# A fused transformer forward pass on one core: delta rule in chunks of 128 tokens, and another deal of the modulation weight pieces

## The chip, the cores and the metric

The kernel is one program on one core of a Trainium2 chip. It is launched once and computes the whole function. The metric is the device time of that launch in microseconds, lower is better. The engines are PE (TensorE, matrix multiply), DVE (VectorE), ACT (ScalarE), POOL (GpSimd) and SP (SyncE, which here issues loads). Each runs its own instruction stream in order; they meet at semaphores.

## The reference

Two blocks run one after the other on 512 tokens of width 1024. The first is a hybrid block (a state space branch, a windowed attention branch, and a feed-forward network with a causal convolution of 3 taps). The second has two layers, each a feed-forward network, a token mixer and another feed-forward network. Its norms are scaled and shifted by a modulation, a matrix-vector product with a 1024 x 9216 matrix for each layer. The token mixer has a gated delta rule (4 heads of 128) beside a sparse attention. The parts that the change touches, cut to what matters:

```
mod = (cond @ ada_w[l] + ada_b[l]).reshape(B, 3, 3, D)

def chunk_gated_delta_rule(q, k, v, g, beta):
    """S_t = a_t S_{t-1}(I - b_t k_t k_t^T) + b_t v_t k_t^T, o_t = S_t q_t, in chunks."""
    C = GDN_CHUNK                                   # 64
    gc = jnp.cumsum(chunks(g), axis=-1)
    decay = exp(where(causal, gc[..., :, None] - gc[..., None, :], -inf))
    lower = where(strict, einsum("nbhcd,nbhsd->nbhcs", kb, kc) * decay, 0)
    u, w = split(triangular_solve(lower, [v * b, k * b * exp(gc)], unit_diagonal=True))
    def step(S, xs):
        v_new = u_i - w_i @ S
        o = (q_i * exp(g_i)) @ S + (q_i @ k_i.T * d_i) @ v_new
        S = S * exp(g_last) + (k_i * exp(g_last - g_i)).T @ v_new
        return S, o
```

The chunk length changes how the sum is grouped and not what it is: the recurrence over tokens is the same for any chunk length.

## The kernel before

All activations stay on the chip, features on the partitions and the 512 tokens along the free axis. The weights come as a stream of units of 128 x 2048 float32 (1 MB) through two buffers. For each unit SP loads `w_raw`, ACT copies it to `w_hi` (`split_unit`, L338), POOL subtracts to get `w_lo` (L331), and PE multiplies in three passes for float32 accuracy (`three_pass`, L344 to L346). The order of the stages is the list `PLAN`; inside a stage every engine has a function of its own (`pe_...`, `act_...`, `dve_...`) whose code order is its instruction order. No scheduler moves anything.

**Feed-forward** (`pe_ffn`, `act_ffn`, `dve_ffn`). The up stage has 22 units of 48 matmuls each, the down stage 16 units of 33 matmuls (every second one finishes a tile of `x`, L1264 or L1266). The first block's feed-forward (`conv` true) has for each up unit two convolutions of three DVE operations each (L1827, L1830), a multiplication (L1423) and a subtraction (L1411). In the other two kinds the up unit has one multiplication (L1428) and one subtraction.

**The modulation** of layer 0 is computed beside the first block's feed-forward, and that of layer 1 beside the first feed-forward of layer 0. Its weights come as 72 pieces of 128 x 1024 (0.5 MB) through the two slots of `ada_w`. ACT issues the load of piece n + 2 (`load`, L1334) once DVE has released piece n (`ada_free`). DVE runs four operations of 128 x 256 for each piece (L1392, L1394, L1396 or L1402) with a wait on each. After two pieces PE sums over the partitions with two small matmuls (L1302). `ada_turns` says how many pieces belong to each unit. It is the table that all three engines read:

```
        if conv:
            n = (2 if u % 11 == 10 else 1) if u < NUP else 3
        else:
            n = 2 if u < NUP + 14 else 0
```

Here NUP is 22 (up units) and NDN is 16 (down units). At a stage's end `modulated` (L1449) turns the sums into the gains and shifts that the next norm uses, and the norm starts at L449.

**The delta rule** (`pe_gdn`, `act_gdn`, `dve_gdn`). `m_U` becomes the transposed inverse of a unit triangular matrix. It starts from blocks of 2, and each step `b` doubles the block length: 16 matmuls L1665, ACT copies (L1803), 16 matmuls L1674 and 16 matmuls L1678, DVE subtractions (L1935, L1937). The last step leaves L1674 out. The matmuls always cover whole blocks of 128 x 128, whatever `b` is; four heads by four blocks of 128 tokens make 16. Then L1684 forms `m_nw`, and the recurrence goes over 8 chunks of 64 tokens. Even chunks lie in partitions 0 to 63 and odd ones in 64 to 127. In each chunk, for each of four heads, PE makes `v_new` (L1698 with 64 rows and 64 columns of the array, L1700 with 128 rows and 64 columns), ACT copies it to `t_vn` (L1811), PE makes the state's increment (L1708) and two parts of the output (L1705, L1710), DVE updates the state `m_S` (L1946, the first time a copy, L1949) and copies the output out (L1951). Behind the recurrence ACT squares the output (L1815), PE sums the squares over the partitions (L1717, 16 matmuls with one moving column), DVE and ACT turn them into factors (L1960 to L1967), and PE spreads these (L1723). The sparse attention stage then starts with a weight unit (L344).

## Time and profile before

| what | value |
|---|---|
| times of three runs, us | 4437.58, 4438.89, 4424.72 |
| median, us | 4437.58 |
| the profiled execution, us | 4410.95 |
| its span in the trace, us | 4409.1 |
| granted PE clock, mean over the span | 0.908 |
| PE busy / DVE / ACT / POOL, us | 4192.4 / 1718.3 / 1382.6 / 1355.5 |

The profiled execution lies 26.6 us under the median of the runs. The span is the time from the first to the last instruction of the trace; 1.9 us of the execution lie around it. The granted clock is a share of 2.4 GHz: 1.00 is 2.4 GHz and 0.50 is 1.2 GHz. Each matmul of plain float32 shows as two instructions in the trace, so 16 of them are x32.

### The profile page before, as it was taken

How to read it: one execution, taken by the hardware profiler on the slowest of the kernel's cores; microseconds unless marked ns; L12 is line 12 of the kernel's file. 1: busy time of each engine (PE TensorE's matmuls, PEld its weight loads, DVE VectorE, ACT ScalarE, POOL GpSimd, SP SyncE). 2: the span in 40 equal slices, each digit the busy share in tenths (PEclk: the TensorE clock that was granted, in tenths of full speed). 3: DMA queues.
4: the chain of work that ended last, by engine and by line, in shares of the span. 5: the costliest groups of instructions: out<-in, count | busy, mean ns of one | idle time of the engine just before them, and what ended most of it. 6: DMA issues, size and time to landing. Idle time of an engine off the chain costs nothing.

```text
span 4409.1 us, 50418 instructions
## 1 busy us (share of the span) xinstructions
PE 4192.4 (95%) x20328; PEld 3448.1 (78%) x20328; DVE 1718.3 (39%) x3207; ACT 1382.6 (31%) x1872; POOL 1355.5 (31%) x298
## 2 busy tenths in 40 slices
PE   7999999999998899999979999999999998899998
PEld 7887888877887788888866678878888886667887
DVE  4767245534765544545334321011103532432110
ACT  4556234433221222233212232232223321222222
POOL 2223432223443344532010034454453201003445
PEclk9999999999998899989965599999998977559999
DMA  3111221112446555721110022332232102002223
GB/s 126 60 66 70 95 86 58 48 58 93 145 155 229 181 185 183 249 89 49 32 45 1 1 86 96 114 106 97 100 129 86 49 6 72 1 1 77 96 105 124
DMA packets 66355, 401.92 MB, mean 91 GB/s; under 512 B 7776, under 2 KB 8288, under 8 KB 27872
## 3 DMA queue, kind: packets, MB, share of 16 engines
q1 hardware_dynamic: 44624, 314.73, 20.2%
q10 hardware_dynamic: 21520, 84.16, 6.1%
q8 instruction: 159, 2.61, 0.2%
q14 instruction: 52, 0.43, 0.0%
HBM read 396.76 MB, written 2.10 MB: 90 GB/s over the span
## 4 chain that ended last, share of the span: by engine, by line
issue 76%; POOL 14%; PE 9%; POOLq 0%; DVE 0%; ACT 0%; DVEq 0%; ACTq 0%
POOL w_lo L331 14%; PE g L344 3%; PE g L346 3%; PE g L345 3%; PE p L405 0%; POOLq L327 0%; DVE x L1463 0%; PE p L429 0%; POOLq L330 0%; POOLq L331 0%; ACT L421 0%; ACT n_sq L413 0%; DVE h_lo L466 0%; DVE n_t L462 0%; ACT h_hi L443 0%
## 5 line engine op out<-in xcount | busy, mean ns | idle before, releaser
L331 POOL TENSOR_TENSOR w_lo<-w_raw,w_hi 128x2048 fp32r<-128x2048 f32 x294 | 1355.3, 4610 | 3043.4 <-ACT w_hi L338 3043.4
L344 PE MATMUL g<-h_hi,w_lo 128*128 128x512 f32 x2848 | 1134.9, 398 | 20.8 <-DVE h_lo L466 12.4
L346 PE MATMUL g<-h_hi,w_hi 128*128 128x512 f32 x2848 | 1116.0, 392 | 0.0
L345 PE MATMUL g<-h_lo,w_hi 128*128 128x512 f32 x2848 | 1115.2, 392 | 0.0
L338 ACT ACTIVATE w_hi<-w_raw 128x2048 fp32r<-128x2048 f32 x294 | 562.6, 1914 | 1236.7 <-PE g L346 1211.1
L344 PEld LDWEIGHTS g<-h_hi,w_lo 128*128 128x128 f32 x2848 | 539.3, 189 | 141.2 <-issue 21.3
L346 PEld LDWEIGHTS g<-h_hi,w_hi 128*128 128x128 f32 x2848 | 538.7, 189 | 115.0
L345 PEld LDWEIGHTS g<-h_lo,w_hi 128*128 128x128 f32 x2848 | 539.6, 189 | 113.4 <-issue 4.1
L344 PE MATMUL g<-act_hi,w_lo 128*128 128x512 f32 x880 | 358.6, 407 | 0.0
L345 PE MATMUL g<-act_lo,w_hi 128*128 128x512 f32 x880 | 352.9, 401 | 0.0
L346 PE MATMUL g<-act_hi,w_hi 128*128 128x512 f32 x880 | 352.8, 401 | 0.0
L1428 DVE TENSOR_TENSOR p<-f_acc,g 128x512 f32<-128x512 f32 x88 | 61.3, 696 | 621.8 <-PE g L346 621.8
L1266 DVE SCALAR_TENSOR_TENSOR x<-g,mods,x 128x512 f32<-128x512 f32 x48 | 36.0, 751 | 475.1 <-PE g L346 475.1
L346 PEld LDWEIGHTS g<-act_hi,w_hi 128*128 128x128 f32 x880 | 168.5, 191 | 40.9
L345 PEld LDWEIGHTS g<-act_lo,w_hi 128*128 128x128 f32 x880 | 169.2, 192 | 38.6
L344 PEld LDWEIGHTS g<-act_hi,w_lo 128*128 128x128 f32 x880 | 169.3, 192 | 38.5
L1394 DVE SCALAR_TENSOR_TENSOR p<-ada_w,csilu,p 128x256 f32<-128x256 f32 x360 | 176.3, 490 | 48.5 <-DMA ada_w<-in_ada 36.5
L2082 PEld LDWEIGHTS p<-m_v,n_pt 128*128 128x128 f32 x640 | 140.2, 327 | 53.9 <-issue 49.1
L2082 PE MATMUL p<-m_v,n_pt 128*128 128x64 f32 x640 | 150.1, 422 | 31.5 <-ACT n_pt L2200 31.5
L2061 PE MATMUL g<-n_k,n_q 64*128 64x128 f32 (+3 forms) x256 | 157.8, 767 | 2.7 <-ACT n_pct L2192 1.6
L2186 ACT ACTIVATE n_p<-g,n_stat 128x128 f32<-128x128 f32 (+3 forms) x128 | 67.4, 527 | 292.6 <-DVE n_stat L2309 292.6
L1359 ACT ACTIVATE f_acc<-g 128x512 f32<-128x512 f32 x88 | 52.8, 600 | 277.5 <-PE g L346 277.5
(390 smaller groups left out, 5347.6 us busy)
## 6 DMA issues: line engine op xcount, KB each, us to landing
w_raw<-in_stream SPq DMA_DIRECT2D x294, 1024.0 KB, 4.8
ada_w<-in_ada ACTq DMA_DIRECT2D x144, 512.0 KB, 4.4
n_w<-in_w ACTq DMA_DIRECT2D x8, 1024.0 KB, 14.1
x<-in_x SPq DMA_DIRECT2D x4, 512.0 KB, 7.1
out_x<-x SPq DMA_DIRECT2D x4, 512.0 KB, 2.6
masks<-in_masks SPq DMA_DIRECT2D x1, 1408.0 KB, 13.2
cols<-in_cols SPq DMA_DIRECT2D x1, 338.0 KB, 13.0
n_pos<-in_pos ACTq DMA_DIRECT2D x1, 256.0 KB, 6.6
```

The lines of the kernel that those rows point to most:

```text
L331: K.nc.gpsimd.tensor_tensor(K.w_lo[:, s], K.w_raw[:, s], K.w_hi[:, s].bitcast(F32), ALU.subtract).then_inc(K.sem("w_lo"), 1)
L338: act.activation(K.w_hi[:, s], K.w_raw[:, s], ACT.Copy).then_inc(K.sem("w_hi"), 1)
L344: nc.tensor.matmul(out, w_lo, h_hi, start=start, stop=False)
L345: nc.tensor.matmul(out, w_hi, h_lo, start=False, stop=False)
L346: return nc.tensor.matmul(out, w_hi, h_hi, start=False, stop=stop)
L1266: v.scalar_tensor_tensor(x, K.g[b][:], gate(m), x, ALU.mult, ALU.add).then_inc(K.sem("x_ready"), 1)
L1359: act.activation(K.f_acc[:, s], K.g[2 * s][:], ACT.Silu).then_inc(K.sem("f_s"), 1)
L1394: v.scalar_tensor_tensor(acc, w, c, acc, ALU.mult, ALU.add).then_inc(pos.own, pos.tick())
L1428: v.tensor_tensor(K.p[s][:], K.f_acc[:, s], K.g[2 * s + 1][:], ALU.mult).then_inc(K.sem("f_u"), 1)
L2061: t.matmul(K.g[2 * (v % 2) + i][:, 0:w], K.n_q[r, j, qb * P:qb * P + P], K.n_k[r, 2 + i, 0:w], start=True, stop=True).then_inc(K.sem("scor ...
L2082: last = t.matmul(K.p[2 + v % 2][:, 64 * i:64 * i + 64], K.n_pt[:, v % 2, 4 * i + k], K.m_v[:, k, P * i + 64 * G:P * i + 64 * G + 64], sta ...
L2186: act.activation(K.n_p[:, v % 2, i * w:i * w + w], K.g[2 * (v % 2) + i][:, 0:w], ACT.Exp, scale=-1.0, bias=s[:, v % 4, i:i + 1], accum_out ...
```

## The change

Two things change. `ada_turns(True)`, the deal for the first block's feed-forward, gives two pieces to each of the 22 up units and the first 12 down units, and one to each of the last four, in place of one (twice two) in the up stage and three in the down stage. The number of pieces stays 72, and the deal of the other feed-forward stays as it is.

The delta rule goes in 4 chunks of 128 tokens. The masks follow (`tri` for `tri64`, `ones` for `bd64`, `causal` for `off64`, a new `inv64`), the inversion has a further step (b = 64; b = 32 becomes a whole step), and the recurrence has 4 passes, all of whose matmuls use 128 rows and 128 columns of the array. The output of all chunks stays in the PSUM banks `g[h]`. It is squared and multiplied from there, so that the copies of L1951 go; the last chunk has no state update; and the sums of squares go to `p[3]`.

```
--- before.py
+++ after.py
@@ -1282,7 +1282,7 @@
     turns, at = [], 0
     for u in range(NUP + NDN):
         if conv:
-            n = (2 if u % 11 == 10 else 1) if u < NUP else 3
+            n = 2 if u < NUP + 12 else 1
         else:
             n = 2 if u < NUP + 14 else 0
...
@@ -1588,9 +1588,9 @@
     def spread(h):
         if h:
             pe.wait_ge(K.sem("m_qe"), pos.next("m_qe"))
-        t.matmul(K.p[0][:], K.mask("off64"), ident.unsqueeze(1).broadcast_to([P, NB, P]), start=True, stop=False)
+        t.matmul(K.p[0][:], K.mask("causal"), ident.unsqueeze(1).broadcast_to([P, NB, P]), start=True, stop=False)
         for c in range(NB):
-            last = t.matmul(K.p[0][:, c * P:c * P + P], K.m_gl[:, c, h:h + 1].broadcast_to([P, P]), K.mask("tri64"),
+            last = t.matmul(K.p[0][:, c * P:c * P + P], K.m_gl[:, c, h:h + 1].broadcast_to([P, P]), K.mask("tri"),
                             start=False, stop=c == NB - 1)
         last.then_inc(K.sem("m_bc"), 1)
...
@@ -1624,8 +1624,8 @@
     unit(0)
     pe.wait_ge(K.sem("m_gl"), pos.next("m_gl"))
     g = K.m_gl[:].rearrange("p c h -> p (c h)")
-    t.matmul(K.p[0][:, 0:16], K.mask("tri64"), g, start=True, stop=True)
-    t.matmul(K.p[1][:, 0:16], K.mask("bd64"), g, start=True, stop=True).then_inc(K.sem("acs"), 1)
...
-    for b in (2, 4, 8, 16, 32):
+    for b in (2, 4, 8, 16, 32, 64):
...
@@ -1668,7 +1668,7 @@
             if b == 2:
                 pe.wait_ge(K.sem(f"g_free{h}"), pos.next(f"g_free{h}"))
             pe.wait_ge(K.sem("m_copied"), pos.next("m_copied"))
-            if b < 32:
+            if b < 64:
                 for c in range(NB):
                     q = slice(c * P, c * P + P)
                     last = t.matmul(K.g[h][:, q], K.m_U[:, h, q], K.t_y[:, h, q], start=True, stop=True)
@@ -1684,37 +1684,28 @@
             last = t.matmul(K.p[h][:, q], K.m_kbe[:, h, q], K.m_U[:, h, q], start=True, stop=True)
         last.then_inc(K.sem("m_raw"), 1)
 
-    for ch in range(8):
-        c, e = ch // 2, ch % 2
-        r = slice(64 * e, 64 * e + 64)
+    for c in range(NB):
         q = slice(c * P, c * P + P)
-        qe = slice(c * P + 64 * e, c * P + 64 * e + 64)
-        o = slice(64 * e, 64 * e + 64)
         for h in range(4):
-            if ch == 0:
-                pe.wait_ge(K.sem("m_copied"), pos.next("m_copied"))
-            else:
-                pe.wait_ge(K.sem("m_st"), pos.next("m_st"))
-            last = t.matmul(K.p[h][r, 0:P], K.m_U[r, h, qe], K.m_vb[r, h, q], start=True, stop=ch == 0)
-            if ch:
-                last = t.matmul(K.p[h][r, 0:P], K.m_nw[:, h, qe], K.m_S[:, h], start=False, stop=True)
+            pe.wait_ge(K.sem("m_st" if c else "m_copied"), pos.next("m_st" if c else "m_copied"))
+            last = t.matmul(K.p[h][:, 0:P], K.m_U[:, h, q], K.m_vb[:, h, q], start=True, stop=c == 0)
+            if c:
+                last = t.matmul(K.p[h][:, 0:P], K.m_nw[:, h, q], K.m_S[:, h], start=False, stop=True)
             last.then_inc(K.sem("m_raw"), 1)
         for h in range(4):
-            if ch:
-                pe.wait_ge(K.sem("m_os"), pos.next("m_os"))
-                t.matmul(K.g[h][:, o], K.m_S[:, h], K.m_qk[:, h, qe], start=True, stop=False)
-        for h in range(4):
+            if c:
+                t.matmul(K.g[h][:, q], K.m_S[:, h], K.m_qk[:, h, q], start=True, stop=False)
             pe.wait_ge(K.sem("m_copied"), pos.next("m_copied"))
-            t.matmul(K.p[h][:, 256:256 + P], K.m_kd[r, h, q], K.t_vn[r, h], start=True, stop=True
-                     ).then_inc(K.sem("m_step"), 1)
-            t.matmul(K.g[h][:, o], K.t_vn[r, h], K.m_at[r, h, qe], start=ch == 0, stop=True
-                     ).then_inc(K.sem("m_step"), 1)
-    pos.skip("m_os", 4)
-    pos.skip("m_st", 4)
+            if c < NB - 1:
+                t.matmul(K.p[h][:, 256:256 + P], K.m_kd[:, h, q], K.t_vn[:, h], start=True, stop=True
+                         ).then_inc(K.sem("m_step"), 1)
+            last = t.matmul(K.g[h][:, q], K.t_vn[:, h], K.m_at[:, h, q], start=c == 0, stop=True)
+            if c == NB - 1:
+                last.then_inc(K.sem("m_os"), 1)
     for h in range(4):
         pe.wait_ge(K.sem("m_osq"), pos.next("m_osq"))
         for c in range(NB):
-            last = t.matmul(K.g[0][:, h * NB + c:h * NB + c + 1], K.m_sq[:, h, c * P:c * P + P], K.mask("ones")[:, 0:1],
...
@@ -1797,22 +1788,20 @@
     for h in range(4):
         act.wait_ge(K.sem("m_raw"), pos.next("m_raw"))
         act.activation(K.t_T[:, h], K.p[h][:], ACT.Copy).then_inc(K.sem("m_copied"), 1)
-    for b in (2, 4, 8, 16, 32):
+    for b in (2, 4, 8, 16, 32, 64):
         for h in range(4):
             act.wait_ge(K.sem("m_raw"), pos.next("m_raw"))
             act.activation(K.t_y[:, h], K.p[h][:], ACT.Copy).then_inc(K.sem("m_copied"), 1)
     for h in range(4):
         act.wait_ge(K.sem("m_raw"), pos.next("m_raw"))
         act.activation(K.m_nw[:, h], K.p[h][:], ACT.Copy, scale=-1.0).then_inc(K.sem("m_copied"), 1)
-    for ch in range(8):
-        r = slice(64 * (ch % 2), 64 * (ch % 2) + 64)
+    for c in range(NB):
         for h in range(4):
             act.wait_ge(K.sem("m_raw"), pos.next("m_raw"))
-            act.activation(K.t_vn[r, h], K.p[h][r, 0:P], ACT.Copy).then_inc(K.sem("m_copied"), 1)
-    pos.skip("m_os", 28)
+            act.activation(K.t_vn[:, h], K.p[h][:, 0:P], ACT.Copy).then_inc(K.sem("m_copied"), 1)
     for h in range(4):
         act.wait_ge(K.sem("m_os"), pos.next("m_os"))
-        act.activation(K.m_sq[:, h], K.m_o[:, h], ACT.Square).then_inc(K.sem("m_osq"), 1)
+        act.activation(K.m_sq[:, h], K.g[h][:], ACT.Square).then_inc(K.sem("m_osq"), 1)
     pos.skip("m_ss", 4)
     act.wait_ge(K.sem("n_ms"), pos.next("n_ms"))
...
@@ -1928,39 +1917,31 @@
         decayed(h)
     for h in range(4):
         v.tensor_tensor(blocks(K.t_m[:, h]), blocks(K.t_l[:, h]), mask("inv2"), ALU.mult).then_inc(K.sem("m_inv"), 1)
-    for b in (2, 4, 8, 16, 32):
+    for b in (2, 4, 8, 16, 32, 64):
         for h in range(4):
-            if b < 32:
+            if b < 64:
                 dve.wait_ge(K.sem("m_step"), pos.next("m_step"))
                 v.tensor_tensor(K.t_T[:, h], K.t_T[:, h], K.g[h][:], ALU.subtract).then_inc(K.sem("m_inv"), 1)
             dve.wait_ge(K.sem("m_step"), pos.next("m_step"))
             v.tensor_tensor(K.m_U[:, h], K.m_U[:, h], K.p[h][:], ALU.subtract).then_inc(K.sem("m_inv"), 1)
-            if b < 32:
+            if b < 64:
                 v.tensor_tensor(blocks(K.t_m[:, h]), blocks(K.t_l[:, h]), mask(f"inv{2 * b}"), ALU.mult
                                 ).then_inc(K.sem("m_inv"), 1)
-    for ch in range(8):
-        c, e = ch // 2, ch % 2
+    for c in range(NB - 1):
         for h in range(4):
             dve.wait_ge(K.sem("m_step"), pos.next("m_step"))
-            if ch:
-                v.scalar_tensor_tensor(K.m_S[:, h], K.m_S[:, h], K.m_el[:, h, ch:ch + 1], K.p[h][:, 256:256 + P],
+            if c:
+                v.scalar_tensor_tensor(K.m_S[:, h], K.m_S[:, h], K.m_el[:, h, c:c + 1], K.p[h][:, 256:256 + P],
                                        ALU.mult, ALU.add).then_inc(K.sem("m_st"), 1)
             else:
                 v.tensor_copy(K.m_S[:, h], K.p[h][:, 256:256 + P]).then_inc(K.sem("m_st"), 1)
-            dve.wait_ge(K.sem("m_step"), pos.next("m_step"))
-            v.tensor_copy(K.m_o[:, h, c * P + 64 * e:c * P + 64 * e + 64],
-                                   K.g[h][:, 64 * e:64 * e + 64]).then_inc(K.sem("m_os"), 1)
-    dve.wait_ge(K.sem("m_os"), pos.next("m_os", 32))
     for h in range(4):
-        x = K.m_o[:, h]
         dve.wait_ge(K.sem("m_osq"), pos.next("m_osq"))
-        v.scalar_tensor_tensor(x, x, K.col2("gdn_norm"), K.m_z[:, h], ALU.mult, ALU.mult
-            ).then_inc(pos.own, pos.tick())
+        v.scalar_tensor_tensor(K.m_o[:, h], K.g[h][:], K.col2("gdn_norm"), K.m_z[:, h], ALU.mult, ALU.mult
+                               ).then_inc(K.sem(f"g_free{h}"), 1)
     dve.wait_ge(K.sem("m_ss"), pos.next("m_ss", 12))
-    v.scalar_tensor_tensor(K.m_f[:], K.g[0][:, 0:16], 1.0 / P / P, K.m_rq2[:].rearrange("p h c -> p (h c)"),
+    v.scalar_tensor_tensor(K.m_f[:], K.p[3][:, 0:16], 1.0 / P / P, K.m_rq2[:].rearrange("p h c -> p (h c)"),
                            ALU.mult, ALU.mult).then_inc(K.sem("n_ms"), 1)
-    for b in range(4):
-        dve.sem_inc(K.sem(f"g_free{b}"), 1)
     dve.wait_ge(K.sem("n_std"), pos.next("n_std"))
     v.reciprocal(K.m_f[:], K.m_f[:]).then_inc(pos.own, pos.tick())
...
@@ -2472,12 +2455,12 @@
 def masks():
     i, j = np.arange(P)[:, None], np.arange(P)[None, :]
     m = {"ident": i == j, "ones": i >= 0 * j, "tri": i <= j, "bd64": i // 64 == j // 64,
-         "tri64": (i <= j) & (i // 64 == j // 64)}
-    for b in (1, 2, 4, 8, 16, 32):
+         }
+    for b in (1, 2, 4, 8, 16, 32, 64):
         m[f"inv{b}"] = (i < j) & (i // b != j // b) & (i // (2 * b) == j // (2 * b))
```

The instruction order on DVE, in the first block's up stage, from the multiplication L1423 of one unit to that of the next (f_acc holds the convolutions, csilu the condition vector). Before:

```order
L1423 TENSOR_TENSOR p<-f_acc,p 128x512
L1392 TENSOR_SCALAR p<-ada_w,csilu 128x256
L1394 SCALAR_TENSOR_TENSOR p<-ada_w,csilu,p 128x256 x2
L1396 SCALAR_TENSOR_TENSOR p<-ada_w,csilu,p 128x256
L1411 TENSOR_TENSOR act_lo<-p,act_hi 128x512
L1827 TENSOR_SCALAR f_acc<-g,cols 128x512
L1830 SCALAR_TENSOR_TENSOR f_acc<-g,cols,f_acc 128x511
L1830 SCALAR_TENSOR_TENSOR f_acc<-g,cols,f_acc 128x510
L1827 TENSOR_SCALAR f_acc<-g,cols 128x512
```

The same place in the changed kernel:

```order
L1423 TENSOR_TENSOR p<-f_acc,p 128x512
L1392 TENSOR_SCALAR p<-ada_w,csilu 128x256
L1394 SCALAR_TENSOR_TENSOR p<-ada_w,csilu,p 128x256 x2
L1396 SCALAR_TENSOR_TENSOR p<-ada_w,csilu,p 128x256
L1394 SCALAR_TENSOR_TENSOR p<-ada_w,csilu,p 128x256 x3
L1402 SCALAR_TENSOR_TENSOR ada_acc<-ada_w,csilu,p 128x256
L1411 TENSOR_TENSOR act_lo<-p,act_hi 128x512
L1816 TENSOR_SCALAR f_acc<-g,cols 128x512
L1819 SCALAR_TENSOR_TENSOR f_acc<-g,cols,f_acc 128x511
L1819 SCALAR_TENSOR_TENSOR f_acc<-g,cols,f_acc 128x510
L1816 TENSOR_SCALAR f_acc<-g,cols 128x512
```

Four more operations of 128 x 256 stand between the multiplication and the subtraction in every unit (L1827 and L1830 are L1816 and L1819 in the changed file).

The instruction order on PE in the recurrence, from the last of a chunk's four heads in the making of v_new to the outputs of the first two heads (m_S is the state, t_vn is v_new). Before, chunk of 64 tokens:

```order
L1698 MATMUL p<-m_vb,m_U 64x128
L1700 MATMUL p<-m_S,m_nw 64x128
L1705 MATMUL g<-m_qk,m_S 128x64 x4
L1708 MATMUL p<-t_vn,m_kd 128x128
L1710 MATMUL g<-m_at,t_vn 128x64
L1708 MATMUL p<-t_vn,m_kd 128x128
L1710 MATMUL g<-m_at,t_vn 128x64
```

In the changed kernel, chunk of 128 tokens:

```order
L1691 MATMUL p<-m_vb,m_U 128x128
L1693 MATMUL p<-m_S,m_nw 128x128
L1697 MATMUL g<-m_qk,m_S 128x128
L1700 MATMUL p<-t_vn,m_kd 128x128
L1702 MATMUL g<-m_at,t_vn 128x128
L1697 MATMUL g<-m_qk,m_S 128x128
L1700 MATMUL p<-t_vn,m_kd 128x128
L1702 MATMUL g<-m_at,t_vn 128x128
```

The state's part of the output (L1705, now L1697) moved from a group of four ahead of the others to the place just ahead of each head's own pair, and every output has 128 columns.

## Rows read from the trace of the kernel before

**Rows 1.** The profile's page, busy time, share of the span and instructions of PE.

```profile
PE 4192.4 (95%) x20328; PEld 3448.1 (78%) x20328; DVE 1718.3 (39%) x3207; ACT 1382.6 (31%) x1872; POOL 1355.5 (31%) x298
```

**Rows 2.** Windows: stretch, length, busy time (instructions) by engine, granted clock, DMA share, GB/s.

```profile
1071.20:1305.30 234.10, 234.10 (x1055) 194.27 (x1054) 168.17 (x260) 66.39 (x65) 97.02 (x21) 1.00 0.42 144
1305.30:1488.00 182.70, 160.21 (x677) 131.37 (x676) 100.60 (x201) 35.29 (x25) 73.55 (x16) 0.88 0.64 224
1515.00:1755.00 240.00, 240.00 (x1097) 199.42 (x1096) 111.27 (x210) 63.58 (x64) 97.03 (x21) 1.00 0.56 183
1755.00:1890.00 135.00, 135.00 (x644) 111.50 (x643) 65.27 (x129) 35.42 (x24) 72.58 (x16) 1.00 0.69 233
```

**Rows 3.** Waits of 1380 to 1560 us: engine, line, releaser, total us, times, longest.

```profile
DVE p L1394 <- DMA ada_w<-in_ada: 20.2, 10, 3.6
```

**Rows 4.** Timeline of DVE, first up stage: start, us, instruction, [idle before, releaser].

```profile
1171.44 0.81 DVE L1827 TENSOR_SCALAR f_acc<-g,cols 128x512 f32<-128x512 f32 x1 [3.06 <-PE g L346]
...
1182.33 0.81 DVE L1827 TENSOR_SCALAR f_acc<-g,cols 128x512 f32<-128x512 f32 x1 [2.58 <-PE g L346]
...
1191.21 1.53 DVE L1830 SCALAR_TENSOR_TENSOR f_acc<-g,cols,f_acc 128x511 f32<-128x511 f32 x2
...
1193.71 0.81 DVE L1827 TENSOR_SCALAR f_acc<-g,cols 128x512 f32<-128x512 f32 x1 [0.97 <-PE g L346]
```

**Rows 5.** Timeline of DVE, first down stage, its start and end.

```profile
1305.01 0.81 DVE L1827 TENSOR_SCALAR f_acc<-g,cols 128x512 f32<-128x512 f32 x1 [2.58 <-PE g L346]
...
1487.34 0.69 DVE L1264 TENSOR_TENSOR x<-x,g 128x512 f32<-128x512 f32 x1 [0.91 <-PE g L346]
...
1500.23 0.19 DVE L449 TENSOR_REDUCE n_ms<-p 128x4 f32<-128x32 f32 x1 [1.03 <-PE p L405]
```

**Rows 6.** Timeline of DVE, second down stage (layer 0), its start and end.

```profile
1757.23 0.70 DVE L1428 TENSOR_TENSOR p<-f_acc,g 128x512 f32<-128x512 f32 x1 [5.54 <-PE g L346]
...
1893.69 0.75 DVE L1266 SCALAR_TENSOR_TENSOR x<-g,mods,x 128x512 f32<-128x512 f32 x1 [12.18 <-PE g L346]
...
1898.78 0.19 DVE L449 TENSOR_REDUCE n_ms<-p 128x4 f32<-128x32 f32 x1 [3.44 <-PE p L405]
```

**Rows 7.** Timeline of PE, two inversion steps of layer 0.

```profile
2079.46 3.74 PE L1665 MATMUL p<-t_T,t_m 128*128 128x128 f32 x32
...
2090.18 3.74 PE L1665 MATMUL p<-t_T,t_m 128*128 128x128 f32 x32
```

**Rows 8.** Timeline of layer 0, recurrence over chunks and what follows it.

```profile
2122.43 1.19 PE L1698 MATMUL p<-m_vb,m_U 64*64 64x128 f32 x8
...
2123.55 0.48 PE L1708 MATMUL p<-t_vn,m_kd 64*128 64x128 f32 x2
...
2124.07 0.29 DVE L1949 COPY m_S<-p 128x128 f32<-128x128 f32 x1 [4.41 <-PE p L1708]
...
2125.48 0.43 PE L1698 MATMUL p<-m_vb,m_U 64*64 64x128 f32 x2
...
2131.32 0.43 PE L1698 MATMUL p<-m_vb,m_U 64*64 64x128 f32 x2
...
2170.22 6.99 PE L1717 MATMUL g<-masks,m_sq 128*128 128x1 f32 x32
...
2178.31 5.66 PE L1723 MATMUL p<-masks,m_fac 128*128 128x128 f32 x32 [1.10 <-DVE m_fac L1967]
...
2183.72 0.48 PE L344 MATMUL g<-h_hi,w_lo 128*128 128x512 f32 x1
```

**Rows 9.** Timeline of PE, layer 1, the same: recurrence's start and next stage's first matmul.

```profile
3556.41 1.19 PE L1698 MATMUL p<-m_vb,m_U 64*64 64x128 f32 x8
...
3631.17 0.48 PE L344 MATMUL g<-h_hi,w_lo 128*128 128x512 f32 x1
```

**Rows 10.** Windows of 20 us: inversion in layer 0, recurrence in layer 1.

```profile
2080.00:2100.00 20.00, 20.00 (x181) 20.00 (x180) 13.30 (x23) 4.78 (x8) 0.00 (x0) 1.00 0.00 1
...
3580.00:3600.00 20.00, 20.00 (x78) 14.64 (x78) 4.35 (x16) 2.11 (x8) 0.00 (x0) 0.50 0.00 1
```

15 lines of the change are left out of this document (10 added, 5 removed).

## The prediction

> **What bounds the kernel now.** I read the page first. PE is busy for 95% of the span, the next engine for 39% [rows 1]. So the question at each place is whether PE is fed, and which work it gets. The windows by stage answer it for the feed-forwards. In the first up stage, the second up stage and the second down stage PE is busy all the time at the full clock of 2.4 GHz (granted 1.00). In the first down stage it is busy for 160.2 of 182.7 us, at a granted clock of 0.88, with DMA at 224 GB/s [rows 2]. The waits name the cause there: DVE waits for modulation pieces to land, ten times and up to 3.6 us each, for L1394 alone [rows 3]. Two slots hold the pieces, a load starts only when its slot is released, and three pieces per unit are more than that pair of slots turns over in a unit. ACT issues the loads in its own order, so the next split waits too, and then PE.
>
> The second place is the delta rule. In the inversion PE passes 181 instructions per 20 us at the full clock. In layer 1's recurrence it passes 78 at a granted clock of 0.50, which is 1.2 GHz [rows 10]. Layer 0 takes 61.3 us from the recurrence's first matmul to the next stage's first (2122.43 to 2183.72) [rows 8]. Layer 1 takes 74.8 us for the same instructions (3556.41 to 3631.17) [rows 9]. PE sets the end in both places, so times on PE are times of the kernel.
>
> **The deal, down stage.** After the change 12 units have two pieces and four have one, 28 in all. The second feed-forward has 28 pieces in the same 16 units, same loads, same matmuls. From the last up unit's end to the last tile of x it needs 136.46 us (1757.23 to 1893.69) [rows 6], the first 182.33 (1305.01 to 1487.34) [rows 5]. The gain is 45.9 us. Behind the last tile come 12.89 us to the next norm's first operation now [rows 5], against 5.09 in the second [rows 6]. Three pieces and their waits stand in between now, and one will; its four operations and two matmuls run beside ACT's last square. I take 5.3 us. That gains 7.6 us.
>
> **The deal, up stage.** A unit with one piece and no sum on PE lasts 10.89 us (1171.44 to 1182.33), one with a sum 11.38 (1182.33 to 1193.71) [rows 4]. Before, 11 sums fell between the first and last up unit, now 21. Ten more at 0.49 us cost 4.8 us. Does DVE keep up? The unit at 1182.33 is one of the two that already have two pieces. DVE ended its chain at about 1192.75 (1191.21 and 1.53) and then waited 0.97 us for PE [rows 4]. So DVE needs 10.42 of 11.38 us, nothing is carried into the next unit, and the extra 20 pieces lie beside PE. The cover is 0.97 us a unit. Without it each unit would cost what exceeds it. The loads run at 183 GB/s in the second up stage, which already has two pieces a unit, and PE is fed [rows 2]. What is queued behind ACT's waits for a free slot is the next unit's silu, whose input comes only at 1192.75. The deal together: 45.9 + 7.6 - 4.8 = 48.7 us.
>
> **The inversion's added step.** Two steps start 10.72 us apart [rows 7], for 48 matmuls, 0.223 us each. b = 32 becomes a whole step and the short last step stays short, so one whole step is added: 10.7 us in each layer, on PE, at the full clock. Masks, `m_el` and the sums' masks change no instruction's size: nothing.
>
> **The recurrence.** All its matmuls become 128 x 128 blocks, as in the inversion; I price them at 0.223 us. The first chunk: 1.12 us until L1708 can start (2122.43 to 2123.55) [rows 8], then eight matmuls, 1.8 us. The two middle ones have 20 each, 4.47 us. The last has 16, 3.57 us. That is 15.4 us. Two waits could stand in between. From a head's product to its copy being ready pass at most 0.9 us (the first chunk's 1.12 less one matmul), and the last head's copy is wanted 2.2 us after its product. The state of the last head has its product started 4.0 us into a chunk and is read 5.8 us after the chunk's start; from product to DVE's start 0.52 us pass (2123.55 to 2124.07) and the operation lasts about 0.3 [rows 8]. Both are hidden. Before, the same part would last 3.05 us (2122.43 to 2125.48) and seven times 5.84 (2125.48 to 2131.32) [rows 8], 43.9 us at the full clock; it lasted 47.8 in layer 0 (to 2170.22), and more in layer 1.
>
> Then the tail. L1717 took 6.99 us [rows 8] at half clock; at the full one I halve it, 3.5 us. ACT's four squares, from PSUM now, overlap the end of the recurrence and each is ready before PE wants it. The chain to the factors is 1.1 us (6.99 after 2170.22, to 2178.31) [rows 8]. L1723 is 16 matmuls, 3.6 us instead of 5.4. Sum: 15.4 + 3.6 + 1.1 + 3.6 = 23.7 us. With the added step 34.4 us. Layer 0 gains 61.3 - 34.4 = 26.9 us, layer 1 74.8 - 34.4 = 40.4 us.
>
> The unknown cost is the price of a matmul in this mix. Its lower bound is the inversion's 0.223 us, its upper that of the old chunk, 5.84 us for 20, 0.292 each [rows 8]. With the upper one the middle chunks stay at 5.84 and the last takes 4.67, 3.8 us more per layer, 7.6 in all. I take the lower: the new matmuls have the inversion's rows and columns of the array, while the old ones alternate between 64 and 128 rows (64*64, 64*128) [rows 8]. The Trainium skill, "TensorEngine Tiling (Array Packing)", Key Properties, says that a change of tiling mode drains the engine. By that rule the old chunk's excess over 20 times 0.223, 1.4 us, is drains, none are left, and the sum stands at the lower value; if the excess came from waits for other engines instead, the sum would be up to 7.6 us smaller. No row before shows which.
>
> The clock: in the trace it was full through the inversion and fell in the recurrence, whose chunk passes 40 instructions in 5.84 us at the full clock, 137 in 20 us, many with 64 rows or columns. The new one has the inversion's 180, so I let it stay full. The tail has 3.5 us of matmuls with one moving column and 1.1 us of nothing, so it may fall there, as it had in layer 0 before (L1717 took 0.44 us per matmul, twice the 0.223). That costs between 0 and 7 us per layer (L1717 and L1723 at twice their time). I take 2 us each.
>
> **The sum.** 48.7 + 26.9 + 40.4 - 4 = 112 us. Against the profiled execution, 4410.95, that gives 4299 us. The median of the runs, 4437.58, lies 26.6 us above that execution. Part of such a spread can be the recurrence itself: its 13.5 us between two layers of equal work are clock alone, and a run in which the clock falls at its start pays more still. What is lost there goes with the change. What is lost elsewhere stays, 4326 us. I take the middle, 4312.
>
> **The rivals**, each counted from 4424, the middle between the execution and the median.
> A. The clock falls in the new recurrence too, at its start. For: it fell in both layers in the old one. Against: the density just named. Then 23.7 us nearly double in both layers, 45 us, 60 with the upper price of a matmul. Gain 56 to 71, time 4353 to 4368.
> B. The first up stage becomes bound by DVE and its loads. For: the cover is only 0.97 us. Against: the unit of [rows 4] has it all. If loads came as late as in the first down stage (182.33 us for 48 pieces, 3.8 each), a unit would last 7.6 us for two pieces and about 6.2 for the convolutions and the rest (10.42 less some 4.2 for two pieces), 13.8, so 22 units lose some 53 us. Gain about 59, time 4365.
> C. The other side: the gaps that such late pieces open let PE's clock fall through the whole up stage, as it did at times in the first down stage (0.88). The 48 matmuls of a unit at 1.2 GHz cost 10.9 us more, 22 units 240. About 4552, slower. It decides from 11 units on. Against: 1.00 in both up stages [rows 2].
> D. Two pieces per unit leave the first down stage bound by loads after all, and half of the 45.9 us stays: 4335. Against it the second down stage moves 233 GB/s and PE is fed [rows 2].
> E. The change does not do what it says: the 112 us cancel against costs not seen, and the time stays within 13 us of before. Both parts would have to fail at once.
>
> The Trainium skill, "TensorE: Matmul & The Clock Gate", HAM oscillation, says that gaps in PE's work bring the throttle back. By that rule A needs gaps that the sum above does not find, and C needs B first; the trace agrees so far, with 0.88 in the stage that waits and 1.00 in the three that do not [rows 2].
>
> **How the numbers follow.** The forecast as summed has 0.75, with its own range 4288 to 4338. A has 0.11, D 0.06, B 0.05, C 0.02, E 0.01. Leaving out the lower and upper ends, 8 in 10 lie from 4286 to 4350; the bounds of the matmul's price (7.6), the tail (up to 10 more) and the median's offset (13 each way) are in it. 0.3%, 13 us, is about what a measurement of this kernel tells from no change. Faster: all but C and E, 0.97. Same 0.01, slower 0.02.
>
> **What would show it.** The first down stage lasts 136 to 138 us, DVE's waits for `ada_w` go, and the granted clock there is 1.00. Up units come every 11.4 us with DVE idle about 1 us in each. There are six inversion steps where there were five, 10.7 us apart. A middle chunk lasts 4.5 us with a granted clock of 1.00, and recurrence plus tail 24 to 27 us in both layers, which become alike. If a middle chunk lasts 5 us or more at the full clock, the price of a matmul was wrong. If the up units last over 11.5, the cover was. If layer 1 still takes 10 us more than layer 0, the clock was.

## The result, and the profile after

| kernel | median, us | lowest to highest (runs) |
|---|---|---|
| before | 4431.15 | 4407.34 to 4438.89 (4) |
| changed | 4298.01 | 4297.66 to 4298.11 (4) |

The ratio is 0.971, with a 95% interval of 0.967 to 0.975: 3% faster. The profiled executions took 4410.95 and 4298.11 us, 112.8 apart. The forecast was 4312 us with a range of 4286 to 4350, and a sum of 112.

The page of the changed kernel, PE's row, answers to [rows 1]. PE is still the bound.

```profile
PE 4104.6 (96%) x20184; PEld 3393.1 (79%) x20184; DVE 1711.2 (40%) x3127; ACT 1378.1 (32%) x1848; POOL 1355.4 (32%) x298
```

Its windows (columns as in [rows 2]): first up stage, first down stage, inversion and recurrence in layer 0, and the tail behind it.

```profile
1069.90:1309.10 239.20, 239.20 (x1094) 198.78 (x1093) 206.46 (x340) 65.77 (x65) 97.00 (x21) 1.00 0.51 183
1309.00:1446.40 137.40, 136.44 (x645) 111.73 (x643) 65.07 (x129) 35.62 (x25) 73.80 (x16) 1.00 0.66 227
2080.00:2100.00 20.00, 19.98 (x180) 19.79 (x178) 6.07 (x16) 6.74 (x21) 0.00 (x0) 1.00 0.00 1
2100.90:2112.00 11.10, 10.00 (x67) 9.92 (x66) 4.87 (x10) 3.78 (x7) 0.00 (x0) 0.69 0.01 1
```

The first down stage lasts 137 us where it had 183, at a clock of 1.00 where it had 0.88. PE passes 180 instructions in 20 us across the end of the inversion and the recurrence, at 1.00; only the tail falls, to 0.69. The timeline of DVE, with the answers to [rows 4] and [rows 5]:

```profile
1138.38 0.81 DVE L1816 TENSOR_SCALAR f_acc<-g,cols 128x512 f32<-128x512 f32 x1 [0.98 <-PE g L346]
...
1149.76 0.81 DVE L1816 TENSOR_SCALAR f_acc<-g,cols 128x512 f32<-128x512 f32 x1 [0.98 <-PE g L346]
...
1309.08 0.81 DVE L1816 TENSOR_SCALAR f_acc<-g,cols 128x512 f32<-128x512 f32 x1 [0.98 <-PE g L346]
...
1323.60 1.54 DVE L1394 SCALAR_TENSOR_TENSOR p<-ada_w,csilu,p 128x256 f32<-128x256 f32 x3 [3.42 <-DMA ada_w<-in_ada]
...
1446.38 0.69 DVE L1264 TENSOR_TENSOR x<-x,g 128x512 f32<-128x512 f32 x1 [7.04 <-PE g L346]
...
1453.16 0.19 DVE L449 TENSOR_REDUCE n_ms<-p 128x4 f32<-128x32 f32 x1
```

Up units come 11.38 us apart, with 0.98 us of idle time on DVE. Its waits for `ada_w`, 72.3 us in 33 before by the view of waits over the whole span, are 11.5 us in 5. The stage lasts 239.2 us (1069.91, the first unit's first tile, to 1309.08), 5.0 more than before (1070.84 to 1305.01). From there to the last tile of x it is 137.30 us, and to the norm 6.78. The timeline of PE answers to [rows 8] and [rows 9]:

```profile
2063.98 3.74 PE L1665 MATMUL p<-t_T,t_m 128*128 128x128 f32 x32
...
2074.70 3.74 PE L1665 MATMUL p<-t_T,t_m 128*128 128x128 f32 x32
...
2085.42 1.34 PE L1691 MATMUL p<-m_vb,m_U 128*128 128x128 f32 x8
...
2092.85 0.39 PE L1691 MATMUL p<-m_vb,m_U 128*128 128x128 f32 x2
...
2097.32 0.39 PE L1691 MATMUL p<-m_vb,m_U 128*128 128x128 f32 x2
...
2100.89 4.53 PE L1708 MATMUL p<-masks,m_sq 128*128 128x1 f32 x32
2106.52 5.60 PE L1714 MATMUL p<-masks,m_fac 128*128 128x128 f32 x32 [1.10 <-DVE m_fac L1948]
...
2111.87 0.48 PE L344 MATMUL g<-h_hi,w_lo 128*128 128x512 f32 x1
```

Inversion steps are 10.72 us apart, and there are six. A middle chunk lasts 4.47 us, the four 15.47, the tail 10.98, together 26.45 us in layer 0 and the same in layer 1 (3495.02 to 3521.47).

The rest is seen best from norm to norm, by the start of L449. One row per execution; the first stretch is the first block's feed-forward, the third and sixth hold the two delta rules.

| profiled execution | us between norms |
|---|---|
| before | 447.2, 398.5, 670.5, 381.2, 382.5, 683.8, 381.1 |
| changed | 401.6, 398.3, 645.9, 381.2, 382.5, 643.0, 381.1 |

### The profile page after: what moved, and what is told of

Its sections match the earlier page's. It is cut to its first block, busy times and chain, and to the rows that moved or that the text cites. A ratio compares the mean times of both kernels' runs of the same rounds, so it can differ in the third digit from the quotient of the medians.

```text
span 4296.3 us, 50018 instructions
## 1 busy us (share of the span) xinstructions
PE 4104.6 (96%) x20184; PEld 3393.1 (79%) x20184; DVE 1711.2 (40%) x3127; ACT 1378.1 (32%) x1848; POOL 1355.4 (32%) x298
## 4 chain that ended last, share of the span: by engine, by line
issue 76%; POOL 14%; PE 9%; POOLq 0%; DVE 0%; ACT 0%; DVEq 0%; ACTq 0%
POOL w_lo L331 14%; PE g L344 3%; PE g L345 3%; PE g L346 3%; PE p L405 0%; POOLq L327 0%; DVE x L1463 0%; PE p L429 0%; POOLq L330 0%; POOLq L331 0%; ACT L421 0%; ACT n_sq L413 0%; DVE h_lo L466 0%; DVE n_t L462 0%; ACT h_hi L443 0%
## 5 line engine op out<-in xcount | busy, mean ns | idle before, releaser
L345 PEld LDWEIGHTS g<-h_lo,w_hi 128*128 128x128 f32 x2848 | 539.4, 189 | 112.8 <-issue 4.1
## 6 DMA issues: line engine op xcount, KB each, us to landing
masks<-in_masks SPq DMA_DIRECT2D x1, 1344.0 KB, 13.2
```

The source lines that it names most:

```text
L345: nc.tensor.matmul(out, w_hi, h_lo, start=False, stop=False)
```

## The experiments

Each group ran beside the kernel before on one chip; the groups ran on different chips.

**One part at a time.** The new line of `ada_turns` in the kernel before, and the old line in the changed one:

```
-            n = (2 if u % 11 == 10 else 1) if u < NUP else 3
+            n = 2 if u < NUP + 12 else 1
```

> The kernel before with the new deal of the modulation pieces alone; the delta rule stays in chunks of 64. My theory: the parts add up. The deal gave 45.5 us between the second norm of the first block and the first norm of layer 0 in the profiled executions (447.2 and 401.6 us), so the profile here shows 402 us for that stretch, a first down stage of 137 us (1309 to 1446), and the median stands 45 to 49 us under the kernel before. The runs spread as before, by 15 to 30 us, since the old recurrence, whose clock I hold responsible, is still in it. Rival one, the gains overlap (the clock or the DMA of one part helps the other): the stretch shows less than 35 us or more than 55. Rival two, the spread of the kernel before came from the three pieces per unit and not from the recurrence: the runs here lie within 2 us of each other.

> The changed kernel with the old deal of the modulation pieces; the delta rule stays in chunks of 128. My theory: 61 to 68 us less than the kernel before, of which 24.6 in layer 0 and 37.7 in layer 1 by the profiled executions (recurrence and tail 26.5 us in both layers, against 61.3 and 74.8), the rest of it the part of the old recurrence's clock that varies from run to run. The runs lie within 2 us of each other. The first down stage stays at 182 us with waits for ada_w of 72 us in all. Rival, the spread comes from the first down stage: the runs here spread by 15 to 30 us.

The deal alone: 4382.50 us (4374.71 to 4385.01, 4 runs) against 4429.38 for the kernel before on that chip (13 runs, 4412.83 to 4439.50), ratio 0.990 (0.987 to 0.993), 46.9 us. The stretch is 401.95 us, the down stage 137.65. The chunks alone: 4342.57 us (4340.82 to 4344.05, 4 runs), ratio 0.981 (0.979 to 0.984), 86.8 us, where I expected 61 to 68. The two gains sum to 133.7 us; the change gave 133.1 between its medians. So the parts add up, and the chunks are worth some 20 us more in a typical run than in the profiled execution. The two sets of runs also say where the spread comes from. With the old recurrence and the new deal it is 10.3 us, less than the 15 to 30 that I expected and far over the 2 of rival two. With the new recurrence and the old deal it is 3.2 us, over the 2 expected and far under the 15 to 30 of the rival. So most of the spread needs the old recurrence.

**The kernel before once more.**

> The kernel before, profiled again. My theory of its run-to-run spread (4407 to 4439 us): it lies in the recurrence, where the clock falls at a place that varies. Then every stretch between norms has the length it had (within 1 us) except the two that hold the delta rule (670.5 and 683.8 us in the first profile), and their difference from the first profile is that of the executions. Rival: the difference lies in the first down stage (447.2 us from norm to norm in the first profile), whose loads can come in another order.

Its eight runs had a median of 4427.09 us (4413.18 to 4435.30). The profiled one took 4418.21 us, 7.3 more than the first profile. From norm to norm: 442.8, 398.2, 683.7, 381.2, 382.3, 683.7, 381.1. Layer 0's stage is 13.2 us longer and the first stretch 4.4 shorter. The timeline of PE in layer 0's recurrence:

```profile
2131.32 0.43 PE L1698 MATMUL p<-m_vb,m_U 64*64 64x128 f32 x2
...
2137.17 0.43 PE L1698 MATMUL p<-m_vb,m_U 64*64 64x128 f32 x2
...
2146.83 0.68 PE L1698 MATMUL p<-m_vb,m_U 64*64 64x128 f32 x2
...
2157.26 0.68 PE L1698 MATMUL p<-m_vb,m_U 64*64 64x128 f32 x2
```

A chunk goes from 5.85 to 10.43 us (2146.83 to 2157.26) once the clock is down. Here it fell in the fifth chunk in both layers. In layer 0 of the first profile it fell only near the end of the recurrence; with the deal alone it fell in the fourth chunk of layer 0. Six such stages took 670.5, 683.8, 683.7, 683.7, 687.9 and 683.7 us, so the first is the exception. The old first stretch varied too: 447.2 and 442.8 in the two profiles of before, 444.2, 451.1, 444.8 and 441.1 in the profiles of four other kernels with the old deal; with the new deal it stayed between 399.5 and 403.9. So the theory that every other stretch keeps its length within 1 us was wrong, and the rival has a share: 4.4 us between two executions of the same kernel, against 13.2 from layer 0's delta rule. Both profiles of before lie under its median of 4429.38. Of the 86.8 us that the chunks gave, the two stages account for 65 by the first profile and for 78 by the second; where the other 8 lie no profile shows.

**What makes an old chunk slow.** Three kernels with 8 chunks whose matmuls cover more of the array. They leave out the limits of a chunk of 64 tokens, so what they compute differs from the reference; their times are what is asked. Full blocks:

```
-            last = t.matmul(K.p[h][r, 0:P], K.m_U[r, h, qe], K.m_vb[r, h, q], ...)
+            last = t.matmul(K.p[h][:, 0:P], K.m_U[:, h, q], K.m_vb[:, h, q], ...)
...
-            t.matmul(K.g[h][:, o], K.t_vn[r, h], K.m_at[r, h, qe], ...)
+            t.matmul(K.g[h][:, 0:P], K.t_vn[:, h], K.m_at[:, h, q], ...)
```

and in the same way for the other three. With full rows only, `r` goes on the side of the operands and `qe` and `o` stay (the first chunk keeps its 64 rows in L1708 and L1710); with full columns only it is the reverse.

> The kernel before, still 8 chunks of 64 tokens, but every matmul of the recurrence (the two of v_new, the two of the output, the state's increment) and the copy of v_new cover 128 rows and 128 columns of the array. What is computed in the recurrence differs from the reference by that; the number of instructions, of waits and their order do not. Theory one, the old chunk's 5.84 us (20 matmuls, 0.292 each) against the new one's 4.47 (0.223 each) is the alternation of 64 and 128 rows and columns: a chunk takes 4.5 us here and the recurrence from its first matmul to the sums of squares 34 to 35 us in place of 47.8 in layer 0. Theory two, the excess is waits for ACT and DVE between the dependent steps, which eight chunks have and four do not show because DVE no longer copies the output out: a chunk stays at 5.8 us. On the clock: if it falls because 64-row matmuls leave the array half used, it stays at 1.00 through the recurrence here and both layers are alike, with runs within 2 us of each other; if it falls for another reason (the number of chunks), it falls at about the same place, to 0.50.

> The kernel before, 8 chunks of 64 tokens, with all its matmuls of the recurrence from chunk 1 on summing over 128 rows of the array (v_new's first product, the state's increment and the second part of the output took 64), while the columns of v_new and the moving columns of the outputs stay 64. What is computed in the recurrence differs from the reference by that. Full blocks throughout gave 4.47 us for a chunk in place of 5.84 and a clock that stayed at 1.00. Theory one, it is the change between 64 and 128 rows that costs: a chunk takes 4.5 us or less here (two of its five kinds of matmuls have fewer moving columns), and the clock stays at 1.00. Theory two, it is the 64 columns: a chunk stays near 5.8 us and the clock falls at about the fourth chunk.

> The kernel before, 8 chunks of 64 tokens, whose matmuls of the recurrence have all 128 stationary and moving columns, while three of its five kinds still sum over 64 rows of the array. What is computed in the recurrence differs from the reference by that. With full rows and the old columns a chunk took 4.71 us, with both full 4.47, with neither 5.84 until the clock fell. Theory one, the alternation of 64 and 128 rows is what costs and what goes with the lower clock: a chunk stays at 5.8 us or more while the clock is full, the clock falls at the fourth or fifth chunk, and the two delta rule stages take 683 us or more from norm to norm. Theory two, rows and columns count alike: a chunk takes about 5.1 us and the clock falls later or not at all, with stages of 655 to 665 us.

| recurrence | chunk, us | two delta rule stages, us | median, us (runs) |
|---|---|---|---|
| old (64 rows and columns) | 5.85, later 10.43 | 670.5 to 687.9 | 4429.38 (13) |
| full columns only | 5.79 | 663.5, 663.4 | 4383.31 (2) |
| full rows only | 4.71 | 652.9, 653.0 | 4359.38 (2) |
| full blocks | 4.47 | 653.1, 653.0 | 4364.14 (4) |

Full blocks do 2.5 times the multiplications (rows times columns times moving columns, over the 20 matmuls) with the same instructions and waits in 4.47 us a chunk. So the 1.37 us over 4.47 were not waits. (The 5 us between its median and that of full rows lie in the old first stretch, 451.1 and 444.8 us.) The rows name the place. Timeline of PE with full columns only, inside a chunk:

```profile
2137.06 0.48 PE L1698 MATMUL p<-m_vb,m_U 64*128 64x128 f32 x2
2137.48 0.49 PE L1700 MATMUL p<-m_S,m_nw 128*128 128x128 f32 x2
2137.89 0.48 PE L1698 MATMUL p<-m_vb,m_U 64*128 64x128 f32 x2
...
2141.00 0.38 PE L1708 MATMUL p<-t_vn,m_kd 64*128 64x128 f32 x2
2141.23 0.38 PE L1710 MATMUL g<-m_at,t_vn 64*128 64x128 f32 x2
2141.45 0.38 PE L1708 MATMUL p<-t_vn,m_kd 64*128 64x128 f32 x2
```

Where matmuls of 64 and 128 rows alternate, they start 0.42 us apart; where two of 64 rows follow each other, 0.22. A change costs 0.19 us here, and 0.17 on the mean of the eight changes of a chunk (5.79 less 4.47). With the old columns it cost 0.14: L1698 and L1700 started 0.36 us apart, and 0.22 with full rows; eight such changes make 1.1 us, the difference between 5.84 and 4.71. The last 0.24 us, from 4.71 to 4.47, go with the 64 columns. That settles the term that the prediction left between two bounds: the alternation of rows is 1.1 of the 1.4 us of excess, and the Trainium skill's rule cited there ("TensorEngine Tiling (Array Packing)", Key Properties) holds with these numbers.

The table also says how much of the chunk change is the chunk length. A stage of 683.7 us becomes 653.1 with full blocks and eight chunks, 30.6 us less, and 643.0 to 646.0 in the changed kernel, 7 to 10 less again: half as many chunks, less the added inversion step. So three quarters or more of the gain of such a stage come from matmuls that all cover the whole array (no change of rows, and a clock that holds), and the smaller part from fewer chunks.

The clock is a second thing. In none of the three did it fall in the profiled recurrence. Windows of the recurrence, full columns only, and the kernel before in layer 0 and twice in layer 1:

```profile
2119.00:2159.00 40.00, 40.00 (x278) 33.23 (x276) 12.19 (x55) 7.76 (x29) 0.00 (x0) 1.00 0.00 1
2126.00:2160.00 34.00, 34.00 (x234) 25.21 (x234) 9.96 (x44) 6.53 (x24) 0.00 (x0) 1.00 0.00 1
3560.00:3578.00 18.00, 18.00 (x124) 13.21 (x122) 5.46 (x24) 3.45 (x13) 0.00 (x0) 1.00 0.00 1
3578.00:3632.00 54.00, 52.90 (x224) 42.08 (x223) 14.65 (x43) 10.17 (x25) 0.00 (x0) 0.53 0.00 1
```

Theory one of the text on full columns was right on the price and wrong on the clock: the alternation is there in full, 5.79 us a chunk, and the clock stayed at 1.00. PE is shown busy all the time in the first three; in layer 1 the clock fell at 3578 us behind 18.00 us without a gap, and the last window has 1.1 us of nothing only in the tail. In the kernel before the weight loads are busy for 25.2 of 34 us, with full columns for 33.2 of 40. The two runs with full columns, 4377.36 and 4389.26, are 12 us apart, and only the first was profiled; their mean granted clocks, 0.914 and 0.913, do not tell whether it fell in the second. What exactly the clock follows stays open.

**The cover of the up stage.**

```
-            n = 2 if u < NUP + 12 else 1
+            n = 3 if u < 24 else 0
```

> The changed kernel with three modulation pieces in each of the 22 up units and the first two down units, none behind them. It asks how far the cover of the up stage reaches. A unit has 11.38 us of matmuls plus 0.25 for half a sum more; DVE needs 10.42 us with two pieces, and about 2.1 more for the third. Theory one, DVE's own work is the bound: units of 12.5 us, the up stage 275 us in place of 239, the down stage about 133, the kernel some 30 us over 4298, and the granted clock stays at or near 1.00. Theory two, the turnover of the two slots is the bound, as in the first down stage before the change (182.7 us for 48 pieces, 3.8 each): a unit lasts three times 3.8 and 6.2, some 17.6 us, the up stage 387 us, and the clock falls in it: over 150 us more.

4373.39 us (2 runs), 70 more than the changed kernel on that chip (below), between the theories. The first stretch took 473.4 us. A unit on DVE, and a window of the stage (columns as in [rows 2]):

```profile
1185.28 0.80 DVE L1816 TENSOR_SCALAR f_acc<-g,cols 128x512 f32<-128x512 f32 x1
...
1196.73 0.49 DVE L1392 TENSOR_SCALAR p<-ada_w,csilu 128x256 f32<-128x256 f32 x1 [1.66 <-DMA ada_w<-in_ada]
...
1199.44 0.80 DVE L1816 TENSOR_SCALAR f_acc<-g,cols 128x512 f32<-128x512 f32 x1
```

```profile
1150.00:1250.00 100.00, 87.81 (x373) 72.31 (x372) 81.22 (x139) 21.24 (x21) 31.71 (x8) 0.91 0.53 184
```

A unit takes 14.2 to 14.7 us, this one 14.16: DVE's own work of 12.5 and a wait of 1.66 for the third piece, since two slots hold two. The clock in the stage fell to 0.91, not further. So the bound is DVE plus one load's rest, and theory two had put all three loads in series. The cover is worth what [rows 4] show: two pieces fit, three cost 3 us a unit.

**The rest of the down stage.** Two other deals:

```
+            n = 2 if u < NUP + 14 else 0                                 # flat
+            n = 1 if NUP <= u < NUP + 2 else 2 if u < NUP + 15 else 0    # late
```

> The changed kernel, whose first feed-forward deals two pieces to each of the first 14 down units and none to the last two, as the second feed-forward does, in place of two to 12 and one to four. My theory: what stood behind the last tile of x in the changed kernel (6.78 us to the next norm, against 5.09 in the second feed-forward) is the last unit's piece, and the down stage has the cover for it elsewhere. The norm starts 5.1 us behind the last tile, the stage from norm to norm goes from 401.6 to 399.9 us, and the kernel to 4296.3 us, 1.7 less. Rival: the two more pieces in units 13 and 14 make a load late there, and the gain is taken back: 4298 us or more.

> The changed kernel again, on the chip of its variant with the other deal. Theory: 4298 us with runs within 1 us of each other, and the stretches between norms as in its first profile within 1 us (401.6, 398.3, 645.9, 381.2, 382.5, 643.0, 381.1 us). Rival: its small spread was chance, and a delta rule stage or the first feed-forward moves by over 3 us.

> The changed kernel with one piece in each of the first two down units, two in each of the next 13 and none in the last (28, as before). In the changed kernel DVE waited for ada_w 0.9, 3.4, 3.0 and 2.8 us in the first four down units, and the first two tiles of x came 0.8 us late against the 17.16 us of the others (2.5 us late in its second profile). My theory: the pieces at the stage's start are late because the down units are shorter than the up units while the loads of the up units are still queued; with one piece there the waits go, the tiles come every 17.2 us from the first, and the empty last unit brings the norm to 5.9 us behind the last tile (as with 14 units of two and two of none). The stage from norm to norm takes 399.5 to 400 us, in place of 401.6 and 403.9. Rival: the waits at the start come from the weights and not from the pieces, the tiles keep their delay, and the stage takes 400.5 us or more.

The changed kernel took 4303.35 us on that chip (4301.89 to 4304.33), the flat deal 4299.50 (4297.08 to 4302.72), the late one on another chip 4297.86 (4296.87 to 4298.82). The first stretch: 403.9, 400.5 and 399.5 us. In the late deal the tiles come 17.16 us apart from the second on and the stage lasts 135.95 us. The waits at its start were the pieces': of the four, 10.2 us in all, one of 1.0 is left at its start. The norm comes 5.98 us behind the last tile, in the flat deal 5.90, where I had expected 5.1 for the latter. There DVE waits for PE's sums (L405), and these took 1.87 us at a granted clock of 0.50 in the flat deal; in the second feed-forward, where 5.09 was read, they took 1.05 at 1.00. Timeline of PE, flat deal:

```profile
1451.03 1.87 PE L405 MATMUL p<-masks,n_sq 128*128 128x1 f32 x8 [4.03 <-ACT n_sq L413]
```

The flat deal's gain of 3.9 us on the changed kernel's chip is more than the 1.7 expected; the first stretch accounts for 3.4 of it, some of which is chance, since it differs by 2.3 between two profiles of the same kernel. For the changed kernel itself my theory, 4298 us within 1 us, missed; the 4298 of the flat deal's two theories counted on it and decide nothing. Between the two profiles of the changed kernel the delta rule stages differ by 3 us each, 645.9 and 643.0, then 642.9 and 646.0; the layer that takes longer has one short fall of the clock more in its sparse attention.

In the changed kernel something else ends last. POOL and DVE behind the last tile there:

```profile
1448.30 4.50 POOL L331 TENSOR_TENSOR w_lo<-w_raw,w_hi 128x2048 fp32r<-128x2048 f32 x1 [4.42 <-ACT w_hi L338]
...
1450.03 0.23 DVE L1449 TENSOR_TENSOR mods<-p,cols 128x72 f32<-128x72 f32 x1 [0.76 <-PE p L1302]
1450.29 2.53 DVE L1452 SCALAR_TENSOR_TENSOR mods<-mods,cols 128x8 f32<-128x8 f32 x1
1452.74 0.16 DVE L1455 TENSOR_SCALAR mods<-mods 128x8 f32<-128x8 f32 x1
```

L1452 works on 128 x 8 and has two operands in SBUF, `mods` and `cols`. It took 2.53 us and ended with POOL's subtraction (1448.30 + 4.50 = 1452.80). In the second profile it took 2.27 us and ended with POOL again (1457.10 against 1457.07); in the flat deal it ran ahead of POOL's and took 0.17. L1449, with an operand in PSUM, ran beside the same subtraction in 0.23 us. The Trainium skill, "SBUF — State Buffer", "SBUF: two separate sides", says that of a DVE operation with two SBUF inputs and a GpSimd operation that reads SBUF the one that starts first locks the other out for the whole instruction; the trace agrees, with DVE's as the second of the two. So the last unit's piece costs more than its own time: it pushes L1452 behind the start of POOL's subtraction. PE's sums had ended at 1451.36, so of the 2.4 us that L1452 lost an estimated 1.7 reached the norm, which would else have come 5.1 us behind the last tile.

**The tail of the delta rule.** The sums of squares with 128 moving columns:

```
-            last = t.matmul(K.p[3][:, h * NB + c:h * NB + c + 1], K.m_sq[:, h, c * P:c * P + P], K.mask("ones")[:, 0:1],
+            last = t.matmul(K.p[h][:, c * P:c * P + P], K.m_sq[:, h, c * P:c * P + P], K.mask("ones"),
```

> The changed kernel, whose 16 sums of squares behind the recurrence take all 128 columns of ones as moving operand in place of one, into the four banks p[h], of which DVE reads every 128th column in four small operations; the values are the same. In the changed kernel these matmuls passed 12 instructions in the first us and 7 in the fourth, where the granted clock had fallen from 1.00 to 0.50, and L1714 behind them took 5.6 us in place of 3.6. Theory one, the clock falls because one-column matmuls leave the array idle most of the time: with 128 columns the sums take 3.6 us, the clock stays at 1.00 until the factors' chain, L1714 takes 3.6 to 4 us, and each layer's tail (from the first sum to the next stage's first matmul) goes from 11.0 to 8.3 us, the kernel 5 us under the changed one. Theory two, it falls for the 1.1 us in which PE has nothing, or for what lies ahead of the sums: the tail stays at 11 us or grows by the 0.8 us that the wider sums cost at the full clock.

Windows of PE in the changed kernel, the first and the fourth us of the sums:

```profile
2100.89:2101.89 1.00, 1.00 (x12) 1.00 0.00 0
2103.89:2104.89 1.00, 1.00 (x7) 0.50 0.00 0
```

4296.90 us (4294.71 to 4299.70, 4 runs). The tail is 8.42 us in layer 0 (2100.75 to 2109.17) and 8.42 in layer 1 where it was 10.98. Timeline of PE:

```profile
2100.75 3.74 PE L1708 MATMUL p<-masks,m_sq 128*128 128x128 f32 x32
2105.58 3.84 PE L1714 MATMUL p<-masks,m_fac 128*128 128x128 f32 x32 [1.09 <-DVE m_fac L1950]
```

L1714 takes 3.84 us in place of 5.60. More columns, less time: theory one. The idle time ahead of L1714 is 1.09 us as before and the clock did not fall for it, against theory two. Not all of the 5.1 us arrive: the two stages take 643.1 and 643.5 us, 2.4 to 2.9 under the 645.9 and 646.0 of the changed kernel and about its 643.0 and 642.9, since this execution has the short fall in the sparse attention in both layers.

**Both gains together.**

> The changed kernel with both edits that gained: one piece in each of the first two down units, two in the next 13, none in the last, and 128 moving columns in the sums of squares. Theory: they lie in different stages and add up. The first feed-forward takes 399.5 to 400 us from norm to norm (the changed kernel: 401.6 and 403.9), each tail from the first sum of squares to the next stage's first matmul 8.4 us (11.0), so about 5.1 and 2 to 4 us less than the changed kernel's two profiled executions (4298.1 and 4303.7): 4291 to 4296 us. Rival: the edits share one gain (the phase in which the clock comes back in later stages moves by some 3 us in one stage or another), and it stays at 4297 us or more like each alone.

4294.85 us (4292.10 to 4295.69, 5 runs) against 4422.32 on that chip, ratio 0.971 (0.969 to 0.973). The first stretch is 399.5 us and the tails 8.42: both gains are there. Against the changed kernel, 4298.0 and 4303.4 us on two other chips, this is 3.2 to 8.5 us, under what a measurement of times alone can tell; only the rows of the two places show it.

## Why the prediction was right, by its own steps

| term | predicted, us | measured, us |
|---|---|---|
| down stage | -45.9 | -45.0 |
| behind the last tile | -7.6 | -6.1 |
| up stage | +4.8 | +5.0 |
| deal, norm to norm | -48.7 | -45.5 |
| inversion, a layer | +10.7 | +10.7 |
| four chunks | 15.4 | 15.47 |
| tail, with its reserve of 2 | 10.3 | 10.98 |
| layer 0 | -24.9 | -24.6 |
| layer 1 | -38.4 | -40.8 |
| elsewhere | 0 | -1.9 |
| sum between executions | -112 | -112.8 |

The deal: reading the second feed-forward as the model of the first was right to 0.9 us. The difference are loads that come late in the first four down units, where the short units follow an up stage that moves 183 GB/s. The 5.3 us behind the last tile missed L1452's wait for POOL. The whole deal gave 45.5, 3.2 less than forecast. Rival B did not come (units of 11.38 us, idle 0.98), nor C; the experiment with three pieces shows that B's price a unit, 13.8 us, would have needed a third piece. D did not come.

The recurrence: the lower price of a matmul, 0.223 us, was right, for the reason given (1.1 us of the old chunk's excess are changes of rows, 0.24 go with the columns). The clock stayed at 1.00, so rival A did not come. In the tail it fell within the sums, as feared: 12 instructions passed in their first us and 7 in the fourth. The reserve of 2 us measured 2.7. The prediction held that the trace agrees so far with the rule that gaps bring the throttle back; its own [rows 10] already spoke against it, with PE busy for 20.00 of 20 us at 0.50, so gaps alone could not weigh rival A.

The 1.9 us elsewhere are 1.5 ahead of the first changed stage and 0.4 behind, in unchanged work. And layer 1 gained 2.4 more than its terms, 3.1 of it in the sparse attention, where the first profile of before had shown a short fall of the clock that the changed kernel's did not.

That the sum of the executions came out to 1 us is in part luck: the deal was 3.2 us short, layer 1 gave 2.4 more than its terms and 1.9 came from elsewhere.

The step that was off is the median. "What is lost there goes with the change. What is lost elsewhere stays, 4326 us. I take the middle, 4312." Nothing stayed. The profiled execution of before lay 18 to 20 us under the medians of 13 and of 4 runs, and the median came down by 133 us where the profiled executions differ by 113. Of these 20 us, 13.2 are layer 0's clock, if a typical run is like the second profile; the others are not located. The changed kernel's runs are 0.5 and 2.4 us apart, so the change removed the spread wherever it lay. The range, 4286 to 4350, had this case at its lower end. Had I taken the executions alone, 4299, the number would have been right to 1 us, with the luck just named.

## What to carry to other kernels

When the runs of a kernel spread by far more than those of its neighbours, ask which stage can vary, and whether the change removes it: then its gain is larger than one profiled execution shows. Small float32 matmuls that alternate between 64 and 128 rows pay 0.14 to 0.19 us at each change on top of 0.22, so that a chunk of 128 tokens with whole blocks (4.47 us) costs less than one of 64 (5.84). Ask first whether all matmuls of a chain can use the same rows, and then how long a chunk should be. A table that deals side work to units should leave the shortest units the fewest pieces, and the last one none.

## What the runs showed of the hardware

A busy PE is no guard of its clock: in layer 1's old recurrence PE is shown busy for all 18.00 us from 3560 to 3578 at a granted clock of 1.00 and for the 20 us of [rows 10] soon behind them at 0.50. It fell during one-column matmuls as well, and stayed when the same 16 had 128 columns. Two executions of the same kernel differed by 13.2 us in one stage from that. And an operation of 128 x 8 on DVE took 2.3 to 2.5 us beside a running POOL operation in place of 0.17, and ended with it, with no semaphore between them.
